# Recurrent block of a hybrid layer: one weight split per head on GpSimd, decay row by broadcast DMA, inverse levels and recurrence a quarter unit later

## The reference

```
q, k, v = silu(causal_dwconv(proj)); q = l2norm(q) * dk**-0.5; k = l2norm(k)
beta = sigmoid(b); g = -exp(A_log) * softplus(a + dt_bias); G = cumsum(g) in a chunk
decay = exp(G_i - G_j) for i >= j
L = strict_lower((k*beta) k^T * decay);  u, w = (I + L)^-1 [v*beta, k*beta*exp(G)]
for each chunk c, with the state S (dk x dv):
    v_new = u_c - w_c S
    o_c   = (q_c exp(G)) S + (q k^T * decay) v_new
    S     = S exp(G_last) + (k exp(G_last - G))^T v_new
o = rmsnorm(o) * norm_g * silu(z)
```

## Time and profile before

| | |
|---|---|
| median of 3 runs | 1401.69 us |
| the profiled execution | 1400.0 us, its span 1398.3 us |
| PE busy | 1331.6 us, 95% |
| DVE, ACT, POOL busy | 795.4 (57%), 579.6 (41%), 259.0 (19%) us |
| DMA, 16 engines | queue q1 27.8%, 111.47 MB in all |
| chain that ended last | PE 75%, DVE 12%, issue 5%, POOL 4%, ACT 4% |

### The profile page before, as it was taken

How to read it: one execution, slowest core, us unless ns; L and a number is a source line. 1 busy time by engine, 2 the same in 40 slices (tenths; PEclk the granted TensorE clock), 3 DMA queues, 4 the chain that set the end, 5 groups by cost and what they waited for, 6 DMA issues and landing times.

```text
span 1398.3 us, 20319 instructions
## 1 busy us (share of the span) xinstructions
PE 1331.6 (95%) x6903; PEld 1053.1 (75%) x6903; DVE 795.4 (57%) x1650; ACT 579.6 (41%) x1007; POOL 259.0 (19%) x481
## 2 busy tenths in 40 slices
PE   6899999999999999999899999999997989999998
PEld 4678778787787878888678888888885657767676
DVE  4657575575756744344466663365645677874522
ACT  4445353453534532232244442244443545555422
POOL 1124041230413300001410000000032443232200
PEclk9999999999999999999899999999999989999999
DMA  5132222322222223333223323333233312222111
GB/s 155 50 88 72 70 69 60 90 60 75 75 60 77 73 76 90 90 105 97 84 67 99 91 82 101 111 96 96 66 101 83 81 43 63 75 61 73 63 49 73
DMA packets 208503, 111.47 MB, mean 80 GB/s; under 512 B 6826, under 2 KB 206793, under 8 KB 208457
## 3 DMA queue, kind: packets, MB, share of 16 engines
q1 hardware_dynamic: 208073, 110.86, 27.8%
q0 software_dynamic: 384, 0.03, 0.0%
HBM read 108.75 MB, written 2.10 MB: 79 GB/s over the span
## 4 chain that ended last, share of the span: by engine, by line
PE 75%; DVE 12%; issue 5%; POOL 4%; ACT 4%; DMA 0%; POOLq 0%; DVEq 0%; ACTq 0%
PE gb L605 62%; POOL Ue L1994 2%; POOL elt L1991 2%; PE gb L1022 2%; PE gd L1022 2%; PE gd L947 1%; DVE selb L1831 1%; ACT whi L1037 1%; PE gd L960 1%; DVE wlo L1399 1%; PE gd L970 1%; DVE kc L1634 1%; DVE act_a L1434 1%; PE gd L617 1%; DVE Lp L1529 1%
## 5 line engine op out<-in xcount | busy, mean ns | idle before, releaser
L605 PE MATMUL gb<-act_a,whi 128*128 128x512 f32 x2800 | 961.7, 404 | 18.7 <-DVE wlo L1399 10.9
L605 PEld LDWEIGHTS gb<-act_a,whi 128*128 128x128 f32 x2800 | 528.9, 189 | 146.4 <-issue 17.3
L605 PE MATMUL gb<-act_a,wlo 128*128 128x512 f32 x1488 | 583.9, 392 | 0.0
L605 PEld LDWEIGHTS gb<-act_a,wlo 128*128 128x128 f32 x1488 | 282.4, 190 | 51.2 <-issue 1.2
L1399 DVE TENSOR_TENSOR wlo<-raw,whi 128x1024 fp32r<-128x1024 f32 x190 | 235.0, 1238 | 140.5 <-ACT whi L1037 139.9
L1037 ACT ACTIVATE whi<-raw 128x1024 fp32r<-128x1024 f32 x212 | 223.2, 1053 | 186.8 <-PE gb L605 157.0
L605 PE MATMUL gb<-act_b,whi 128*128 128x512 f32 x304 | 109.2, 389 | 0.0
L2081 POOL TENSOR_TENSOR wlo<-raw,whi 128x1024 fp32r<-128x1024 f32 x22 | 53.3, 2422 | 135.1 <-ACT whi L1037 135.1
L605 PEld LDWEIGHTS gb<-act_b,whi 128*128 128x128 f32 x304 | 57.1, 188 | 11.9
L2047 POOL TENSOR_TENSOR zs<-zs,ca 128x512 f32<-128x512 f32 x3 | 5.4, 1786 | 323.8 <-ACT ca L1040 323.8
L2004 POOL TENSOR_TENSOR rr<-ss,rr 128x4 f32<-128x4 f32 x8 | 1.6, 201 | 287.3 <-DVE ss L1602 287.3
(11 more groups left out here) (420 smaller groups left out, 1524.8 us busy)
## 6 DMA issues: line engine op xcount, KB each, us to landing
raw<-in_w_in_dram SPq DMA_DIRECT2D x103, 512.0 KB, 3.6
raw<-in_w_up_dram SPq DMA_DIRECT2D x44, 512.0 KB, 3.6
raw<-in_w_down_dram SPq DMA_DIRECT2D x16, 384.0 KB, 3.2
raw<-in_w_down_dram SPq DMA_DIRECT2D x16, 320.0 KB, 3.1
raw<-in_w_a_out_dram SPq DMA_DIRECT2D x8, 512.0 KB, 3.4
raw<-in_w_b_out_dram SPq DMA_DIRECT2D x8, 512.0 KB, 3.4
raw<-in_w_o_dram SPq DMA_DIRECT2D x8, 512.0 KB, 3.4
raw<-in_w_out_dram SPq DMA_DIRECT2D x8, 512.0 KB, 3.5
```

The source lines that it names most:

```text
L605: ins = pe.matmul(gb[:, b, :], l, r, start=(first and m == 0), stop=(last and m == len(todo) - 1))
```

## The change

1. The split of the fifth unit of each head goes from VectorE (3,2) to GpSimd (`fifth_split`), which does it after `head_b` of the head before and ahead of `head_a`. VectorE's next split, at (4,1), waits for it.
2. Step -1 (L665) goes for heads 1 to 7. In head 0, TensorE turns all 32 rows of G once, ScalarE copies them to `Lp`, SyncE writes them to DRAM; in each later head SyncE reads one row back, broadcast over 128 partitions, straight into `dec`, ahead of the load of unit 2's weights. L1513 reads `dec` in SBUF instead of PSUM.
3. Inverse levels (12 to 17) and recurrence (19 to 29) are renumbered one up: each comes a quarter later on all engines. The output's square is step 31 at (2,3), the multiplication by its inverse root step 32, still at (3,0) on VectorE; the turn becomes step 34, at (3,2) on TensorE, (3,3) on ScalarE and VectorE. `head_columns` goes from (2,1) to (2,2).
4. TensorE's step 0 waits for the last output of the head before (`o_ready`).

```diff
             def head_loads(h):
                 for s in range(8):
+                    if s == 2 and not (isinstance(h, int) and h == 0):
+                        sp.wait_ge(lt_ready, 2 * h)
+                        sp.dma_start(flat(dec), g_dram[ds(h, 1), :].to_broadcast([P, T])).then_inc(g_landed, 16)
                     load(N_B + 8 * h + s, N_B + s, w_in_v[:, :, column(B_COLS[s] - 3 * P)])
...
             head_loads(0)
+            sp.wait_ge(g_rows, 1)
+            sp.dma_start(g_dram[:, :].rearrange("h (c i) -> (h c) i", c=TC),
+                         flat(Lp)[0:HEADS * TC, :]).then_inc(g_kept, 16)
+            sp.wait_ge(g_kept, 16)
...
                 elif g == 0:
                     pe.wait_ge(conv_silu, 3 * h + 2)
+                    if not (isinstance(h, int) and h == 0):
+                        pe.wait_ge(o_ready, 4 * h)
...
-                elif g == 12:
+                elif g == 13:
...
-                elif 19 <= g <= 29:
-                    c = (g - 18) // 3
-                    what = (g - 18) % 3
+                elif 20 <= g <= 30:
+                    c = (g - 19) // 3
+                    what = (g - 19) % 3
...
-                        if s == 3 and m == 1 and not peeled:
-                            step(32, h - 1)
+                        if s == 3 and m == 2 and not peeled:
+                            step(34, h - 1)
...
-                        if (s, m) == ((3, 0) if peeled else (2, 3)):
+                        if peeled and (s, m) == (2, 1):
+                            pe.wait_ge(gcum_sb, 1)
+                            pe.transpose(gd[0:HEADS * TC, 3, 0:P], sm[:, 5, 0:HEADS * TC], ident[:]).then_inc(g_turned, 1)
+                        if peeled and (s, m) == (3, 0):
+                            pe.wait_ge(g_rows, 1)
                             step(-1, h)
...
                         if m == 3 and s == 2:
+                            if not peeled:
+                                step(31, h - 1)
                             sc.activation(warm[:], mhalf[:], ACT.Exp)
...
                 if g == 0:
-                    dve.wait_ge(gb_done, h + 1)
-                    link(dve.tensor_tensor(dec[:], bank(gd[:, 3, :]), wide(hc[:, C_G:C_G + TC]), ALU.subtract))
+                    if isinstance(h, int) and h == 0:
+                        dve.wait_ge(gb_done, 1)
+                        src = bank(gd[:, 3, :])
+                    else:
+                        dve.wait_ge(hc_ready, h + 1)
+                        dve.wait_ge(g_landed, 16 * h)
+                        src = dec[:]
+                    link(dve.tensor_tensor(dec[:], src, wide(hc[:, C_G:C_G + TC]), ALU.subtract))
...
                         if late and m == 1 and s != 3:
+                            if s == 4:
+                                dve.wait_ge(split_ready, N_B + 8 * h + 5)
                             split(N_B + 8 * h + s + 1, N_B + s + 1)
...
-                        if s == 2 and m == 1:
+                        if s == 2 and m == 2:
                             head_columns(h)
+                        if s == 2 and m == 3 and not peeled:
+                            step(31, h - 1)
                         if s == 3 and m == 0 and not peeled:
-                            step(31, h - 1)
+                            step(32, h - 1)
                         if s == 3 and m >= 2:
                             shuffles(m)
-                        if s == 3 and m == 2:
-                            split(N_B + 8 * h + s + 1, N_B + s + 1)
                         if s == 3 and m == 3 and not peeled:
-                            step(32, h - 1)
+                            step(34, h - 1)
...
+            def fifth_split(h):
+                n = N_B + 8 * h + 4
+                pool.wait_ge(hi_ready, n + 1)
+                pool.tensor_tensor(wlo[:, (N_B + 4) % 2, :], raw[:, (N_B + 4) % 4, :], whi[:, (N_B + 4) % 2, :].bitcast(F32),
+                                   ALU.subtract).then_inc(split_ready, 1)
+
+            fifth_split(0)
             head_a(0)
             with pool.Fori(1, HEADS) as h:
                 own.enter(h - 1, 3)
                 head_b(h - 1)
+                fifth_split(h)
                 head_a(h)
```

More of the change, by code:

```diff
@@ L363, in hybrid_block_kernel @@
         gb_done = sem("gb_done")
+        g_turned = sem("g_turned")
+        g_rows = sem("g_rows")
+        g_kept = sem("g_kept")
+        g_landed = sem("g_landed")
         arg_ready = sem("arg_ready")
@@ L706, in step @@
                     ins.then_inc(y_done, 1)
-                elif g == 13:
+                elif g == 14:
                     pe.wait_ge(zeros_ready, 1)
@@ L714, in step @@
                     ins.then_inc(z_done, 1)
-                elif g == 14:
+                elif g == 15:
                     pe.wait_ge(zeros_ready, 1)
@@ L723, in step @@
                     ins.then_inc(y_done, 1)
-                elif g == 15:
+                elif g == 16:
                     pe.wait_ge(zeros_ready, 1)
@@ L731, in step @@
                     ins.then_inc(z_done, 1)
-                elif g == 16:
+                elif g == 17:
                     pe.wait_ge(zeros_ready, 1)
@@ L740, in step @@
                     ins.then_inc(y_done, 1)
-                elif g == 17:
+                elif g == 18:
                     pe.wait_ge(zeros_ready, 1)
@@ L833, in _ @@
                     elif j == 3 and m == 2:
-                        step(32, HEADS - 1)
+                        step(34, HEADS - 1)
                 for _ in u:
@@ L1179, in head @@
                             step((s - 3) * 4 + m, h)
-                        elif not peeled:
+                        elif not peeled and (s, m) != (2, 3):
                             step(20 + s * 4 + m, h - 1)
-                        if s == 3 and m == 2 and not peeled:
-                            step(32, h - 1)
+                        if peeled and (s, m) == (2, 2):
+                            sc.wait_ge(g_turned, 1)
+                            sc.activation(flat(Lp)[0:HEADS * TC, :], gd[0:HEADS * TC, 3, 0:P], ACT.Copy).then_inc(g_rows, 1)
+                        if s == 3 and m == 3 and not peeled:
+                            step(34, h - 1)
                         if s == 4 and m == 3:
@@ L1526, in step @@
                     dve.wait_ge(lt_ready, 2 * h + 1)
+                    if isinstance(h, int) and h == 0:
+                        dve.wait_ge(g_kept, 16)
                     for b in range(P // B):
```

27 lines of the change are left out of this document (14 added, 13 removed).

## The result

The changed kernel takes 1419.44 us (median of 4 runs, 1418.72 to 1420.62) against 1401.55 of the kernel before (4 runs beside them, 1399.2 to 1402.76): ratio 1.0134, 95% interval 1.0122 to 1.0145. The forecast was 1417, slower. The profiled execution took 1419.24.

What follows compares the result with a forecast made beforehand. PE, busy 56.80 of 58.80 us a turn, was taken as the bound. Added 5.56 less removed 3.37 gave +2.2 a turn, +15.3 over seven, head 0 even, recurrence of head 7 +0.1: 1417 us, range 1411 to 1421.

Steps and rivals of the forecast that it cites:

- Unit 4's split: GpSimd's split, ready at X + 5.93 against 9.85, removes a 1.23 us wait per turn but holds up VectorE.
- L779 late by 0.95, L682 by 1.98: Unit 3 into 4: VectorE's L1605 waits behind GpSimd's split, delaying PE's output turn and L682; 2.93 us a turn.
- VectorE first: Rival: L1605 goes before GpSimd's split, L1518 waits, L779 on time, L682 loses 1.41; 1406 us, chance 0.17.
- the hold-up does not bind: Rival: GpSimd's split does not hold VectorE up, 2.68 against 3.37 a turn; 1395 us, chance 0.19.
- all handoffs fit: Rival: no handoff is late after the moves, 27 us saved; 1375 us, chance 0.05.
- Unit 1: L754 0.13 late behind the state copy, L766 0.89 late because Rr follows the q taps; 1.02 us a turn.
- L729 0.27, L738 1.34: Units 6 and 7: inverse levels late behind VectorE's L1650 and a later unit's split; 1.61 us a turn.
- L704 in the loop: Unit 6: due 1.4 us later, elimination begins about 3 later, PE itself 3 behind; nothing lost, within 0.3.
- the rival of a late elimination: Rival: elimination also late, 0.3 to 1 us a turn at L704; 1420 to 1424 us, chance 0.09.
- The turn: One head-loop turn, 58.80 us before, was to lengthen by 2.2, to 61 us.
- the 3.37 removed: Per-turn saving: 1.0 for L665's matmuls, 1.23 for unit 4's wait, 1.14 for waits at L704 and L738.
- Head 0: Saves 3.06 before unit 4 and 0.3 at L738, pays 1.6 at L729 and L738, about 1.7 at L704: 0.

Runs made afterwards that it cites:

- The kernel with VectorE first: Changed kernel, but in heads 1 to 7 GpSimd's split waits until VectorE has multiplied the output (L1638): 1427.63 us, ratio 1.0194.
- the shift alone: Changed kernel without GpSimd's split and the decay row, leaving the quarter shift of inverse levels and recurrence: 1423.14 us, ratio 1.0147 to the kernel before.
- the reordered kernel: Changed kernel's shift and decay row, fifth split on VectorE behind the exponent, orders mended where PE waits: 1381.4 us, ratio 0.9862 to the kernel before.
- GpSimd's split alone: Kernel before with only the fifth split moved to GpSimd, ahead of the elimination: 1401.02 us, ratio 1.0002.
- the right side ahead of the taps: Changed kernel, but at (1,1) VectorE makes the right side Rr before the convolution taps of q: 1417.27 us, ratio 1.0126.
- the split behind the level: Changed kernel, but in unit 7 VectorE does its split after step 16 instead of before it, in all heads: 1417.14 us, ratio 1.0112.
- the split back on VectorE: Changed kernel with the fifth split back on VectorE at (3,2) and GpSimd's removed, shift and decay row kept: 1436.44 us, ratio 1.0243.

## Why the prediction was right

The forecast's mechanism held, step by step. That the total fell into the range of 1411 to 1421 is in part luck: the sum has no term for the clock, and the experiments above show kernels with the same or shorter waits that lose up to 25 us to it in the loop, where after loses 3.

- **Unit 4's split.** It was to be ready in time and to cost what it holds up. The wait is gone and L1638 takes 2.89 us.
- **L779 late by 0.95, L682 by 1.98** (now L794, L697). Idles of 0.71 and 1.93. The chain between them is as it was worked out: the small instructions late beside L1544 and L1545, the split straight behind them, VectorE second. The rivals "VectorE first", "the hold-up does not bind" and "all handoffs fit" fell here.
- **Unit 1.** 0.89 for L766 (now L781) behind the taps of q: idle 0.57, worth 0.81 when it was taken away. The 0.13 at L754 shows no idle.
- **L729 0.27, L738 1.34** (now L744, L753): idles of 0.25 and 1.40 to 1.43.
- **L704 in the loop**: no wait, as said; the rival of a late elimination fell.
- **The turn**: 61.0 was forecast, 61.31 measured. The terms were delays, and an idle shows less than the delay costs, as the working had it for the wait of unit 4: 0.57 was worth 0.81. With these 0.24 more for each of the five, which is an estimate from the one place where it was measured, 4.89 + 1.2 = 6.1 was added where 5.56 was forecast; less the 3.37 removed that is 2.7, and the turns say 2.51 against the 2.2 of the forecast. By this reckoning the term furthest off is L753's, 1.43 + 0.24 = 1.67 instead of 1.34; by the experiment that removed it, it is 1.5. L744's is 0.49 instead of 0.27 and L697's 2.17 instead of 1.98.
- **Head 0** was to come out even. L719 waits 1.0 instead of the 1.7 forecast, L753 1.64, and the first L753 comes at 90.78 where the first L738 of before came at 90.42: 0.36 later. But L753 stands a quarter further on in the weight stream. ScalarE's splits in the plain units behind the loop follow each other in 5.44 us, a unit of 24 matmuls, so a quarter is 1.36: at the same place of the stream head 0 is 1.0 us ahead of before, and the forecast of no change was off by that.
- **Not in the forecast**: the first loop turn is 64.36 us long, 3.05 more than the others. The windows view of after, behind head 0's L753:

```profile
94.00:98.00 4.00, 4.00 (x14) 3.21 (x13) 0.50 (x2) 0.50 (x1) 0.00 (x0) 0.50 0.00 0
```

The granted clock is at half, its level of 1.2 GHz, after PE has been idle for 1.64 us. The kernel with VectorE first has the same idle there (1.65) at full clock, and its first turn is 60.86. From the last L753 to the end of the span, on the other hand, it takes 1.7 us less than before, where I had 0.1 more; 1.36 of that is the same quarter, and 0.3 stays unexplained. The sum of what was measured is 0.36 + 7 x 2.51 + 3.05 - 1.7 = 19.3, and the profiled runs differ by 1419.24 - 1400.0 = 19.2, where 15.4 was forecast.

Where the loss comes from, by undisturbed turns: 58.80 before, 60.3 with the shift alone, 60.72 with the decay row as well, 61.31 with GpSimd's split on top. On the kernel before, the last two do nothing each. So the shift carries most of the loss, 1.5 of 2.51 us a turn, through orders on VectorE and ScalarE that it leaves alone, and the reordered kernel, which has the shift and turns of 56.64, shows that the shift need not cost anything.

What stays open is which idle brings the clock down. In the kernel before, in the one with GpSimd's split alone and in the reordered one, no idle of a turn is over 1.05 us, and the clock is full in all 21 turns. In the others it is not the length of the idle that tells: behind the same 1.93 us before L697 the clock fell in 0 of 7 turns of after, in 4 of 7 with the right side ahead of the taps, and in 7 of 7 with the split behind the level. So my numbers for single experiments, which held the clock at after's level, missed by up to 20 us in four of them, while three of these four had the waits that were expected. That the lower clock takes the rest is shown for the profiled runs by their windows and by turns of two lengths in one run. For the runs that were only timed only the mean granted clock is on record, and it goes with the time: 0.967 at 1442.7 us and 0.973 at 1429.15 with the split back on VectorE, 0.975 at 1423.55 and 0.981 at 1417.32 with the shift alone, 0.983 in all four runs of after.

## What to carry to other kernels

When steps are moved against each other, write down for each engine the order of instructions around the new place, and ask of each one that is now ahead of a needed one how long it holds it: three such orders cost this kernel more than the idle that the change removed. Before giving work to GpSimd, look at what VectorE does for the length of it: here a two-input instruction and a tensor_scalar were held until the split was over, and a sum was not. On a kernel bound by TensorE, compare the turns of a loop one by one before believing a small difference: here turns of two lengths were a matter of clock, and the turn at full clock told what the edit did. Look at the clock as well as at the length, for in one of these kernels every turn was disturbed.

## What the hardware did that was not expected

- The granted clock fell to half for some 3 or some 7 us after PE had been idle for 1.4 to 3.1 us, in some turns and not in others of the same program. A long stretch costs 3.0 to 3.1 us (63.32 against 60.29 in the shift alone, 63.94 against 60.86 with VectorE first), a short one up to 1.6 (62.10 against 60.49 with the right side ahead of the taps). With the split back on VectorE a turn of 63.9 has two short stretches, behind L753 and before unit 4, and one of 65.4 a long and a short one.
- With VectorE first, an instruction of VectorE on four elements a partition was held until the end of GpSimd's split: L1549 took 1.95 us instead of 0.17. GpSimd's own small ones are late beside VectorE's two-input instructions: 0.57 instead of 0.20, 1.46 instead of 1.01.
- An idle of 0.57 us on PE was worth 0.81 us of time.
